# The low parts of the stick-breaking queries and keys: from VectorE to GpSimd

## The chip, the cores and the metric

The kernel runs on one core of a Trainium2 chip. A core has five engines that run side by side and meet only at semaphores: TensorE (PE in the profile, with its weight loads as PEld), VectorE (DVE), ScalarE (ACT), GpSimd (POOL) and SyncE (SP), which here only issues DMAs. The metric is the device time of one launch in microseconds (us); less is better.

## The reference

One decoder layer on 1024 tokens of width 1024. Attention has two groups of heads beside each other: 8 stick-breaking heads of 64 columns and 4 softmax heads (multi-head latent attention, MLA). The change touches the stick-breaking heads:

```python
z = einsum('bthd,bshd->bhts', q_block, k[:, :kend]) * 64 ** -0.5
strict = s_idx < t_idx
log_beta = log_sigmoid(z)
log_1m = where(strict, log_sigmoid(-z), 0.0)
after = cumsum(log_1m, reverse=True) - log_1m
w = where(strict, exp(log_beta + after), 0.0)
out_block = w @ v[:, :kend]
```

All is float32. The output projection and a SwiGLU feed-forward layer follow.

## The kernel before

Products with float32 accuracy are made of rounded parts. ScalarE copies an operand into a tile of type fp32r (the high part), and another engine subtracts that from the operand (the low part). Three products of parts, or for the 64-column stick heads two products with stacked parts, then stand for one.

The attention stage works in units. A unit is one head and one block of 128 queries; BLOCKS says how many blocks of 128 keys it meets (1, 7, 3, 5, 6, 4, 8, 2, in this order, for each head). 16 units make a pair of heads. First come the 32 MLA units (2 pairs), then the 64 stick units (4 pairs). For each stick unit:

- TensorE makes the scores into PSUM (stick_scores, L1681 and L1682) from headQ, headKH and headKL;
- ScalarE makes omb = sigmoid(-z) (L783) and beta = sigmoid(z) (L791);
- VectorE makes left, a running product of omb (the scan of L1243), then beta = beta * left (the multiply of L1248), both on SBUF tiles;
- TensorE transposes beta (L1722), ScalarE copies it out (L727), TensorE multiplies with the values (L1735), and VectorE copies the output out of PSUM every fourth unit (L1234).

TensorE runs in the order: scores of unit n + 2, transposes of n, values of n - 1.

Each pair of heads needs its queries and keys in parts before its first unit. ScalarE writes pairQH (L735) and pairKH (L739) into one set of tiles; VectorE writes pairQL (L1186) and pairKL (L1190). For pair 0 this happens at unit 12 of the last MLA pair (SPLIT0), queries and keys together. For pairs 1 to 3 it happens during the pair ahead, queries at its unit 4 (SB_Q), keys at its unit 6 (SB_K), behind that unit's own work. SP's stack_head (L369 to L376) waits for all four parts (s_h and s_l) and copies them with five DMAs per head into headQ, headKH and headKL. TensorE waits for the DMAs (head_in) at the first unit of a head. For pairs 1 to 3, SP issues only after the scores of unit 7 (head 0) or 15 (head 1) of the pair ahead.

GpSimd has little to do here: it zeroes the other half of headKL (L522) and the first column of left (L525), and comes back only when the attention is over (L530).

Of the kernel before, what the change touches and what calls it, by code (L numbers as in the profile page):

```python
# [19 lines left out]
ALU = mybir.AluOpType  # L20
# [8 lines left out]
SBH, SBD = 8, 64  # L29
# [74 lines left out]
SB_Q, SB_K, SB_OUT = 4, 6, 11  # L104
# [5 lines left out]
def build(nc, xT, cols_d, rows_d, grow_d, pos_d, ada1_d, ada2_d, win_d, qup_d, kvup_d, wout_d, gu_d, down_d, x2_d, t_d, out_d):  # L110
# [3 lines left out]
    def at(name, shape, dt, kb):  # L114
        return nc.alloc_sbuf_tensor_at(name, shape, dt, offset=base + int(kb * 1024))
# [39 lines left out]
    qkT = at("qkT", [P, 8, S], F32, 34)  # L155
# [45 lines left out]
    pairQH = at("pairQH", [P, S], F32R, 106)  # L201
    pairQL = at("pairQL", [P, S], F32R, 110)
    pairKH = at("pairKH", [P, S], F32R, 114)
    pairKL = at("pairKL", [P, S], F32R, 118)
# [68 lines left out]
    sem = {n: ctx.enter_context(nc.semaphore(n)) for n in names}  # L273
# [53 lines left out]
    def repeat(eng, n, body):  # L327

        if n == 1:
            body(0)  # L330
        else:
            with eng.Fori(0, n) as i:
                body(i)
# [123 lines left out]
    @block.gpsimd  # L457
    def _(pool):
        for n in ("q_r", "rk_done"):
            pool.sem_inc(sem[n], PRIME)  # L460
        k = 0

        def fill(ins):
            nonlocal k
            ins.then_inc(sem["pool_const"], 1)
            k += 1

        fill(pool.memset(ident[:], 0.0))
        fill(pool.memset(identb[:], 0.0))
        fill(pool.memset(mask_sb[:], 0.0))  # L470
        fill(pool.memset(mask_mla[:], 0.0))
        fill(pool.memset(ones[:], 1.0))
        fill(pool.memset(nhalf[:], -0.5))
        pool.wait_ge(sem["pool_const"], k)
        for m in (ident, identb):
            fill(pool.affine_select(out=m[:], in_=m[:], compare_op=ALU.not_equal, fill=1.0, base=0, pattern=[[-1, P]], channel_multiplier=1))

        fill(pool.affine_select(out=mask_sb[:], in_=mask_sb[:], compare_op=ALU.is_gt, fill=NEG, base=0, pattern=[[1, P]], channel_multiplier=-1))
        fill(pool.affine_select(out=mask_mla[:], in_=mask_mla[:], compare_op=ALU.is_ge, fill=NEG, base=0, pattern=[[1, P]], channel_multiplier=-1))

        def rsqrt(k, row, t0=0, t1=NT):

            pool.wait_ge(sem["stat_ms"], k + 1)
            nc.gpsimd.tensor_tensor(rms[:, row, t0:t1], ms[:, row, t0:t1], nhalf[:, t0:t1], ALU.pow).then_inc(sem["stat_r"], 1)

        pool.wait_ge(sem["pool_const"], k)
        rsqrt(0, 0)

        for j in range(KD):
            pool.wait_ge(sem["hH_done"], j + 1)  # L490
            nc.gpsimd.tensor_tensor(hL[:, j, :], x_in[:, j, :], hH[:, j, :], ALU.subtract).then_inc(sem["hL_done"], 1)

        pool.wait_ge(sem["hL_done"], KD)
        pool.memset(acc2[:], 0.0).then_inc(sem["ada_acc"], 1)

        for k, (a, b) in enumerate(((0, 1), (0, 2), (1, 2))):
            pool.wait_ge(sem["low_sq"], (2, 3, 5)[k])
            if k:
                pool.wait_ge(sem["low_add"], k)
            nc.gpsimd.tensor_tensor(sql[a][:], sql[a][:], sql[b][:], ALU.add).then_inc(sem["low_add"], 1)  # L500
        rsqrt(1, 1)
        rsqrt(2, 2)

        def head_rsqrt(i):
            for u in range(2):
                tt = 2 * i + u
                pool.wait_ge(sem["q_ms"], tt + 1)
                nc.gpsimd.tensor_tensor(rstd[:, u, 0:4], qms[:, u, 0:4], nhalf[:, 0:4], ALU.pow).then_inc(sem["q_r"], 1)  # L508
                pool.wait_ge(sem["k_ms"], tt + 1)
                nc.gpsimd.tensor_tensor(rstd[:, u, 4:9], qms[:, u, 4:9], nhalf[:, 0:5], ALU.pow).then_inc(sem["rk_done"], 1)  # L510
        repeat(pool, NT // 2, head_rsqrt)

        pool.wait_ge(sem["low_over"], 1)
        for e in range(2):
            o = 64 * (1 - e)
            pool.memset(KRH[e][o:o + 64, :].bitcast(F32), 0.0).then_inc(sem["kr_zero"], 1)
            pool.memset(KRL[e][o:o + 64, :].bitcast(F32), 0.0).then_inc(sem["kr_zero"], 1)

        for e, u in ((0, NU + 7), (1, 2 * NU - 1)):
            pool.wait_ge(sem["m_qk"], after(u))  # L520
            o = 64 * (1 - e)
            pool.memset(headKL[e][o:o + 64, :].bitcast(F32), 0.0).then_inc(sem["sk_zero"], 1)  # L522
            pool.wait_ge(sem["sk_zero"], e + 1)
        for s in range(2):
            pool.memset(left[s][:, 0:1], 1.0).then_inc(sem["left_one"], 1)  # L525
        pool.wait_ge(sem["left_one"], 2)

        for tt in range(NT):
            pool.wait_ge(sem["o_ms"], tt + 1)
            nc.gpsimd.tensor_tensor(ors[:, ORDER0[tt], :], oms[:, ORDER0[tt], :], nhalf[:, 0:2], ALU.pow).then_inc(sem["o_r"], 1)  # L530

        pool.wait_ge(sem["mix_l"], NT)
        pool.memset(sqa[:], 0.0).then_inc(sem["sqa_zero"], 1)
        for hf in range(2):
            rsqrt(3 + hf, 3, 4 * hf, 4 * hf + 4)

        for hf in range(2):
            if hf == 0:
                pool.wait_ge(sem["g_mm"], NQ * NSU)
                pool.wait_ge(sem["x2_spill"], 16)  # L540
            else:
                pool.wait_ge(sem["y_done"], KD)
            pool.dma_start(xres[:], x2_d[:, :, 512 * hf:512 * hf + 512].rearrange("j p n -> p j n")).then_inc(sem["xres_in"], 16)
            for o in range(KD):
                pool.wait_ge(sem["y_done"], hf * KD + o + 1)
                pool.dma_start(out_d[o, :, 512 * hf:512 * hf + 512], yst[:, o, :]).then_inc(sem["y_out"], 16)
            pool.wait_ge(sem["y_out"], 16 * KD * (hf + 1))
# [382 lines left out]
    def _(dve):  # L930
        for n in ("q_free", "kr_free", "work_done", "t_dve", "m_max", "m_nm", "m_tv", "m_o", "s_scan", "s_wd", "s_o", "t_done", "ll_done", "x2_done", "sqa_done"):
            dve.sem_inc(sem[n], PRIME)
        V = nc.vector
# [247 lines left out]
                n0, n = G0[v] * P, BLOCKS[v] * P  # L1181
                V.tensor_copy(pmT[v % 2][:, n0:n], ps[:, 5, 0:n - n0]).then_inc(sem["m_tv"], 1)

        def stick_q(p):
            dve.wait_ge(sem["s_h"], 2 * p + 1)
            V.tensor_tensor(pairQL[:], qkT[:, p, :], pairQH[:], ALU.subtract).then_inc(sem["s_l"], 1)  # L1186

        def stick_k(p):
            dve.wait_ge(sem["s_h"], 2 * p + 2)
            V.tensor_tensor(pairKL[:], qkT[:, 4 + p, :], pairKH[:], ALU.subtract).then_inc(sem["s_l"], 1)  # L1190

        def maxima(done, recips):

            return min(done, NM) + recips + PRIME
# [10 lines left out]
        def mla_step(u):  # L1205

            p, v = divmod(u, NU)
            n = BLOCKS[v] * P
            dve.wait_ge(sem["m_qk"], after(u))
            V.reduce_max(mx[:, v:v + 1], pair(2 * (v % 2), n), axis=AX.X).then_inc(sem["m_max"], 1)  # L1210
            dve.wait_ge(sem["m_max"], maxima(u + 1, max(0, u - 3)))
            V.tensor_scalar(nmx[:, v:v + 1], mx[:, v:v + 1], -(QK ** -0.5), None, ALU.mult).then_inc(sem["m_nm"], 1)
            if u >= 2:
                mla_copy((u - 2) // NU, (u - 2) % NU)
            if u >= 3:
                mla_finish(u - 3)
            if v == SPLIT1:
                mla_split(p, 1)
            if v == SPLIT0:
                if p == 0:  # L1220
                    mla_split(1, 0)
                else:
                    stick_q(0)
                    stick_k(0)

        def stick_output(u):

# [8 lines left out]
        def stick_step(u):  # L1236

            i, v = divmod(u, NU)
            last = i == SBH // 2 - 1
            n = BLOCKS[v] * P  # L1240
            dve.wait_ge(sem["s_nb"], after(u))
            dve.wait_ge(sem["s_wd"], after(u - 2))
            V.tensor_tensor_scan(left[v % 2][:, 1:n], omb[v % 2][:, 0:n - 1], omb[v % 2][:, 0:n - 1], 1.0, ALU.mult, ALU.bypass).then_inc(sem["s_scan"], 1)  # L1243
            if u < 2:
                mla_copy(MH // 2 - 1, NU - 2 + u)
            dve.wait_ge(sem["s_b"], after(u))
            dve.wait_ge(sem["s_scan"], after(u))
            V.tensor_tensor(beta[v % 2][:, 0:n], beta[v % 2][:, 0:n], left[v % 2][:, 0:n], ALU.mult).then_inc(sem["s_wd"], 1)  # L1248
            if u < 3:
                mla_finish(NM - 3 + u)  # L1250
            else:
                stick_output(u - 3)
            if v == SB_Q and not last:
                stick_q(i + 1)
            if v == SB_K and not last:
                stick_k(i + 1)
            if last and SB_OUT <= v < SB_OUT + 2:
                wsplit(H_OUT + v - SB_OUT, H_OUT + v - SB_OUT)

# [17 lines left out]
        for tt in range(NT + 1):  # L1277
# [6 lines left out]
            if tt >= 1:  # L1284
                k = tt - 1
# [719 lines left out]
```

## Time and profile before

| | |
|---|---|
| median of 3 runs | 1446.08 us (1443.46 to 1449.19) |
| the profiled execution | 1443.19 us |
| its span, first to last instruction | 1441.20 us |
| TensorE busy | 1326.0 us, 92% |
| VectorE busy | 833.1 us, 58% |
| ScalarE busy | 547.3 us, 38% |
| GpSimd busy | 84.5 us, 6% |
| mean granted TensorE clock | 0.971 |
| the stick-breaking stage | about 461 to 634 us of the span |

A timeline row reads: start, duration, engine, line of the kernel, operation, output <- inputs, how many, and in brackets the idle time before it with what ended it. An instruction may be issued before the one ahead has drained, so neighbours can overlap by 0.1 us. "issue" means that the wait isn't explained by what the profile records of engines; a wait for a DMA can hide there.

### The profile page before, as it was taken

Reading aid. Unit: us, or ns where it says so; the run is one execution under the profiler, and the core shown is the slowest. Engines: PE = TensorE matmul, PEld = TensorE weight load, DVE = VectorE, ACT = ScalarE, POOL = GpSimd, SP = SyncE. Lnnn points to the kernel's source line nnn. Section 1 sums busy time; section 2 is a strip of 40 time slices with the busy share of each in tenths; the row PEclk is TensorE's granted clock in tenths of the full one; section 3 lists DMA queues with packets and bytes.
Section 4 is the critical chain, followed back from the end, with each engine's and each line's share of the span. In section 5 each row is a group of like instructions: output and inputs, shape, how many; then the busy total and the mean of one; then the engine's idle time right before and its main releaser. Section 6 shows DMA issues by size and latency. Waiting matters only on the chain.

```text
span 1441.2 us, 17190 instructions
## 1 busy us (share of the span) xinstructions
PE 1326.0 (92%) x6624; PEld 1107.3 (77%) x6624; DVE 833.1 (58%) x1225; ACT 547.3 (38%) x883; POOL 84.5 (6%) x82
## 2 busy tenths in 40 slices
PE   2899999887989898969989999999999999999998
PEld 1688878776877777768867788888888877887886
DVE  8633354477565998865368755666566633334333
ACT  3522312356444776852136333333333322323231
POOL 1600200132000000010000000000000000001001
PEclk9799999899999999979999999999999999999999
DMA  9053423000003323500122122222222225446443
GB/s 383 31 212 124 161 102 121 15 0 1 1 1 74 76 50 74 183 30 17 57 99 106 74 88 88 88 88 88 88 74 74 72 77 201 154 137 242 161 146 124
DMA packets 37404, 143.47 MB, mean 100 GB/s; under 512 B 4176, under 2 KB 4304, under 8 KB 35792
## 3 DMA queue, kind: packets, MB, share of 16 engines
q1 hardware_dynamic: 34992, 134.03, 27.5%
q0 software_dynamic: 2336, 8.39, 1.6%
q8 instruction: 52, 0.85, 0.3%
q14 instruction: 24, 0.20, 0.0%
HBM read 112.00 MB, written 19.92 MB: 92 GB/s over the span
## 4 chain that ended last, share of the span: by engine, by line
PE 71%; DVE 16%; issue 6%; ACT 3%; POOL 2%; DMA 1%; DVEq 0%; SPq 0%; ACTq 0%; POOLq 0%
PE ps L1905 26%; PE ps L1517 15%; PE ps L1506 8%; PE ps L1508 8%; PE ps L1507 8%; DVE left L1243 5%; PE ps L1713 2%; DVE acc L995 1%; DVE beta L1248 1%; PE ps L1702 1%; POOL rstd L508 1%; PE ps L1735 1%; PE ps L1722 1%; DMA t_spill_d<-tst 1%; PE ps L1822 1%
## 5 line engine op out<-in xcount | busy, mean ns | idle before, releaser
L1506 PE MATMUL ps<-TH,dWH 128*128 128x512 f32 x352 | 137.8, 391 | 7.2 <-DVE dWL L1474 6.3
L1507 PE MATMUL ps<-TL,dWH 128*128 128x512 f32 x352 | 137.7, 391 | 0.0
L1508 PE MATMUL ps<-TH,dWL 128*128 128x512 f32 x352 | 137.6, 391 | 0.0
L1905 PE MATMUL ps<-h2H,slH 128*128 128x512 f32 x320 | 124.6, 389 | 2.4 <-ACT s L900 2.4
L1905 PE MATMUL ps<-h2L,slH 128*128 128x512 f32 x320 | 124.5, 389 | 0.0
L1905 PE MATMUL ps<-h2H,slL 128*128 128x512 f32 x320 | 124.5, 389 | 0.0
L1472 DVE TENSOR_TENSOR TL<-traw,TH 128x512 fp32r<-128x512 f32 x44 | 30.5, 693 | 138.6 <-ACT TH L921 138.6
L883 ACT ACTIVATE slH<-ssum 128x512 fp32r<-128x512 f32 x80 | 50.4, 632 | 146.3 <-PE ps L1905 96.2
L1243 DVE TENSOR_TENSOR_SCAN left<-omb 128x127 f32<-128x127 f32 (+3 forms) x64 | 86.3, 1348 | 13.7 <-ACT omb L783 13.7
L921 ACT ACTIVATE TH<-traw 128x512 fp32r<-128x512 f32 x44 | 27.8, 631 | 168.9 <-PE ps L1508 156.8
L974 DVE TENSOR_TENSOR WL<-raw,WH 128x1024 fp32r<-128x1024 f32 x30 | 38.3, 1280 | 85.9 <-ACT WH L561 85.9
L1506 PEld LDWEIGHTS ps<-TH,dWH 128*128 128x128 f32 x352 | 66.5, 189 | 22.3 <-issue 7.1
L1517 PE MATMUL ps<-hH,WH 128*128 128x512 f32 x256 | 79.6, 392 | 0.0
L1517 PE MATMUL ps<-hL,WH 128*128 128x512 f32 x256 | 78.9, 389 | 0.0
L1517 PE MATMUL ps<-hH,WL 128*128 128x512 f32 x256 | 78.8, 389 | 0.0
L1508 PEld LDWEIGHTS ps<-TH,dWL 128*128 128x128 f32 x352 | 66.5, 189 | 13.8
L1507 PEld LDWEIGHTS ps<-TL,dWH 128*128 128x128 f32 x352 | 66.4, 189 | 13.8
L1735 PE MATMUL ps<-VS,wT 128*128 128x64 f32 x576 | 75.1, 278 | 0.0
L1735 PEld LDWEIGHTS ps<-VS,wT 128*128 128x128 f32 x576 | 73.4, 201 | 0.0
L1905 PEld LDWEIGHTS ps<-h2H,slH 128*128 128x128 f32 x320 | 60.1, 188 | 15.3 <-DVE slL L1419 2.8
L1905 PEld LDWEIGHTS ps<-h2L,slH 128*128 128x128 f32 x320 | 60.1, 188 | 12.4
L1905 PEld LDWEIGHTS ps<-h2H,slL 128*128 128x128 f32 x320 | 60.1, 188 | 12.4
(296 smaller groups left out, 3021.3 us busy)
## 6 DMA issues: line engine op xcount, KB each, us to landing
ada<-ada SPq DMA_DIRECT2D x12, 2048.0 KB, 8.1
draw<-down SPq DMA_DIRECT2D x44, 512.0 KB, 3.6
sraw<-gu SPq DMA_DIRECT2D x20, 1024.0 KB, 5.9
traw<-t_spill_d SPq DMA_DIRECT2D x44, 256.0 KB, 3.8
t_spill_d<-tst SPq DMA_DIRECT2D x20, 512.0 KB, 3.0
raw<-win SPq DMA_DIRECT2D x18, 512.0 KB, 3.7
x_in<-xT SPq DMA_DIRECT2D x4, 1024.0 KB, 8.5
headKH<-pairKH SPq DMA_DIRECT2D x16, 256.0 KB, 4.9
```

Source lines behind the costliest of these rows:

```text
L883: A(slH[q][:], operand(u, q), ACT.Copy).then_inc(sem["g_h"], 1)
L921: A(TH[d % 2][:], traw[d % 2][:], ACT.Copy).then_inc(sem["th_done"], 1)
L974: V.tensor_tensor(WL[par % 2][:], raw[r % 2][:], WH[par % 2][:], ALU.subtract).then_inc(sem["split_l"], 1)
L1243: V.tensor_tensor_scan(left[v % 2][:, 1:n], omb[v % 2][:, 0:n - 1], omb[v % 2][:, 0:n - 1], 1.0, ALU.mult, ALU.bypass).then_inc(sem["s_sca ...
L1472: V.tensor_tensor(TL[d % 2][:], traw[d % 2][:], TH[d % 2][:], ALU.subtract).then_inc(sem["tl_done"], 1)
L1506: mm(out, lh, rh, start=first, stop=False)
L1507: mm(out, lh, rl, start=False, stop=False)
L1508: return mm(out, ll, rh, start=False, stop=last)
L1517: last = mm(ps[:, b + hf, :], l[s][:, j * P:(j + 1) * P], r[:, j, 512 * hf:512 * hf + 512], start=(j == 0 and k == 0), stop=(j == KD - 1 a ...
L1713: last = mm(ps[:, 6 + v % 2, 0:VD], pmT[v % 2][:, k * P:(k + 1) * P], VM[:, qt + k, (2 * i + e) * VD:(2 * i + e + 1) * VD], start=(k == 0) ...
L1735: last = mm(ps[:, bank, c:c + SBD], wT[v % 2][:, k * P:(k + 1) * P], VS[:, qt + k, (2 * i + e) * SBD:(2 * i + e + 1) * SBD], start=(k == 0 ...
L1905: last = mm(ps[:, Q_BANK[q], :], l[q][:, w], r[:, c, :], start=(c == 0 and k == 0 and q not in (Q_G2, Q_S4)), stop=(c == 3 and k == 2), sk ...
```

## The change

The two helper functions of VectorE, stick_q and stick_k, and their calls are gone. GpSimd gets stick_lows(p): for the queries and then the keys of pair p it waits for ScalarE's high part and subtracts. Pair 0's are made right after the first headKL memset, pairs 1 to 3's after the left memsets, each as soon as its high part is there. ScalarE, SP and TensorE are untouched; SP still waits for the same counts of s_l.

```diff
+        def stick_lows(p):
+
+            for k, (lo, hi, x) in enumerate(((pairQL, pairQH, qkT[:, p, :]), (pairKL, pairKH, qkT[:, 4 + p, :]))):
+                pool.wait_ge(sem["s_h"], 2 * p + k + 1)
+                nc.gpsimd.tensor_tensor(lo[:], x, hi[:], ALU.subtract).then_inc(sem["s_l"], 1)
+
         for e, u in ((0, NU + 7), (1, 2 * NU - 1)):
             pool.wait_ge(sem["m_qk"], after(u))
             o = 64 * (1 - e)
             pool.memset(headKL[e][o:o + 64, :].bitcast(F32), 0.0).then_inc(sem["sk_zero"], 1)
             pool.wait_ge(sem["sk_zero"], e + 1)
+            if e == 0:
+                stick_lows(0)
         for s in range(2):
             pool.memset(left[s][:, 0:1], 1.0).then_inc(sem["left_one"], 1)
         pool.wait_ge(sem["left_one"], 2)
+        for p in range(1, SBH // 2):
+            stick_lows(p)
...
-        def stick_q(p):
-            dve.wait_ge(sem["s_h"], 2 * p + 1)
-            V.tensor_tensor(pairQL[:], qkT[:, p, :], pairQH[:], ALU.subtract).then_inc(sem["s_l"], 1)
-
-        def stick_k(p):
-            dve.wait_ge(sem["s_h"], 2 * p + 2)
-            V.tensor_tensor(pairKL[:], qkT[:, 4 + p, :], pairKH[:], ALU.subtract).then_inc(sem["s_l"], 1)
-
...
             if v == SPLIT0:
                 if p == 0:
                     mla_split(1, 0)
-                else:
-                    stick_q(0)
-                    stick_k(0)
...
-            if v == SB_Q and not last:
-                stick_q(i + 1)
-            if v == SB_K and not last:
-                stick_k(i + 1)
```

## Rows read from the trace of the kernel before

**Rows 1.** The page's first part: busy time of each engine.
```profile
PE 1326.0 (92%) x6624; PEld 1107.3 (77%) x6624; DVE 833.1 (58%) x1225; ACT 547.3 (38%) x883; POOL 84.5 (6%) x82
```
**Rows 2.** VectorE's timeline in the stick-breaking stage.
```profile
473.35 1.75 DVE L1243 TENSOR_TENSOR_SCAN left<-omb 128x767 f32<-128x767 f32 x1
475.20 0.96 DVE L1248 TENSOR_TENSOR beta<-beta,left 128x768 f32<-128x768 f32 x1
476.08 1.22 DVE L1186 TENSOR_TENSOR pairQL<-qkT,pairQH 128x1024 fp32r<-128x1024 f32 x1
...
479.14 2.28 DVE L1243 TENSOR_TENSOR_SCAN left<-omb 128x1023 f32<-128x1023 f32 x1
481.53 1.23 DVE L1248 TENSOR_TENSOR beta<-beta,left 128x1024 f32<-128x1024 f32 x1
...
483.01 1.21 DVE L1190 TENSOR_TENSOR pairKL<-qkT,pairKH 128x1024 fp32r<-128x1024 f32 x1
...
486.73 2.02 DVE L1243 TENSOR_TENSOR_SCAN left<-omb 128x895 f32<-128x895 f32 x1 [0.65 <-ACT omb L783]
...
506.30 2.02 DVE L1243 TENSOR_TENSOR_SCAN left<-omb 128x895 f32<-128x895 f32 x1 [1.27 <-ACT omb L783]
...
527.00 2.02 DVE L1243 TENSOR_TENSOR_SCAN left<-omb 128x895 f32<-128x895 f32 x1 [0.65 <-ACT omb L783]
...
569.74 2.02 DVE L1243 TENSOR_TENSOR_SCAN left<-omb 128x895 f32<-128x895 f32 x1 [2.87 <-ACT omb L783]
```
**Rows 3.** The chain that ended last: start, us, what ran on it.
```profile
476.08 1.22 DVE pairQL L1186
...
481.53 1.24 DVE beta L1248
482.81 1.09 PE ps L1722 x8
```
**Rows 4.** VectorE's timeline at places where GpSimd also worked.
```profile
39.44 2.34 DVE L1021 TENSOR_TENSOR x_in<-x_in,ps 128x1024 f32<-128x1024 f32 x2
...
42.47 2.73 DVE L995 SCALAR_TENSOR_TENSOR acc<-ada,silu_c,acc 128x512 f32<-128x512 f32 x1
...
147.16 1.65 DVE L974 TENSOR_TENSOR WL<-raw,WH 128x1024 fp32r<-128x1024 f32 x1 [8.10 <-ACT WH L561]
...
167.98 2.58 DVE L974 TENSOR_TENSOR WL<-raw,WH 128x1024 fp32r<-128x1024 f32 x1 [6.01 <-ACT WH L561]
```
**Rows 5.** GpSimd's timeline at the same places.
```profile
39.78 2.37 POOL L491 TENSOR_TENSOR hL<-x_in,hH 128x1024 fp32r<-128x1024 f32 x1 [14.60 <-ACT hH L579]
42.11 2.54 POOL L491 TENSOR_TENSOR hL<-x_in,hH 128x1024 fp32r<-128x1024 f32 x1
...
145.32 2.41 POOL L500 TENSOR_TENSOR sql<-sql,sql 128x1024 f32<-128x1024 f32 x1 [72.77 <-ACT sql L602]
147.87 3.19 POOL L500 TENSOR_TENSOR sql<-sql,sql 128x1024 f32<-128x1024 f32 x1
...
167.08 2.40 POOL L500 TENSOR_TENSOR sql<-sql,sql 128x1024 f32<-128x1024 f32 x1 [16.02 <-ACT sql L602]
```
**Rows 6.** SP's timeline: the last copy issued for head 0.
```profile
455.21 1.23 SPq L376 DMA_DIRECT2D headKL<-pairKL  x1
```
**Rows 7.** headKL's view between 455 and 456 us: that copy alone.
```profile
DMA to landing us min/median/max: 6.0/6.0/6.0
```
**Rows 8.** TensorE's timeline: the first matmul of the stick-breaking stage.
```profile
461.26 0.30 PE L1681 MATMUL ps<-headKH,headQ 128*128 128x128 f32 x1 [2.50 <-issue]
```
**Rows 9.** ScalarE's timeline: the high parts for pair 1.
```profile
473.31 1.09 ACT L735 ACTIVATE pairQH<-qkT 128x1024 fp32r<-128x1024 f32 x1
...
478.74 1.06 ACT L739 ACTIVATE pairKH<-qkT 128x1024 fp32r<-128x1024 f32 x1
```
**Rows 10.** VectorE's timeline: the low part of pair 0's queries.
```profile
449.60 1.22 DVE L1186 TENSOR_TENSOR pairQL<-qkT,pairQH 128x1024 fp32r<-128x1024 f32 x1 [0.98 <-ACT pairQH L735]
```
**Rows 11.** Windows: busy time and count of each engine, PEclk, DMA share, GB/s.
```profile
562.00:564.00 2.00, 0.71 (x4) 0.66 (x4) 1.94 (x3) 0.28 (x1) 0.00 (x0) 0.62 0.03 8
```

## The prediction

> **What bounds the kernel now.** I read the page's first part first: TensorE (PE) is busy 92% of the span, VectorE (DVE) 58%, GpSimd (POOL) 6% [rows 1]. That is a mean over stages, so the stage that the change touches has to be read by itself. In VectorE's timeline of the stick-breaking stage [rows 2] the reader sees that one scan starts when the multiply before it ends and the multiply when its scan ends: 473.35 + 1.75 = 475.10, multiply at 475.20, and so on. VectorE has hardly a gap in eight units, and the chain of waits goes through its scans and multiplies, and through pairQL at 476.08 [rows 3]. So this stage is VectorE's. The one place where it is not is the end of each run of eight units: the multiply of 1024 columns at 481.53 is followed on the chain by PE's transposes (482.81), values and scores, ScalarE's (ACT) sigmoid omb, and only then VectorE's scan at 486.73, which has waited 0.65 us for omb [rows 2, 3]. Between 482.76 and 486.73 VectorE has slack.
>
> At the entrance of the stage something else rules. PE's first stick matmul is at 461.26, after 2.50 us for which no engine is named [rows 8]. The last copy of head 0's operands was issued at 455.21 and took 6.0 us to land [rows 6, 7]: 455.21 + 6.0 = 461.2. PE waits for that DMA, which waits for both low parts.
>
> **The change part by part.**
>
> *Two subtractions leave VectorE in each of three pairs.* I take the start of the 895-column scan as the mark of a run of eight units [rows 2]. 486.73 to 506.30, without low parts: 19.57 us. 506.30 to 527.00, with both: 20.70 us. The difference is 1.13 us, about one subtraction and not two. pairQL (1.22 us, 1.14 start to start) is on the chain. pairKL at 483.01 lies in the slack behind the 1024 multiply: it costs nothing now. So the removal gives 3 x 1.13 = 3.4 us, and only for the query parts.
>
> *The same subtractions on GpSimd.* Its subtractions and additions of 128x1024 f32 take 2.40 us alone (167.08) [rows 5], twice VectorE's 1.22. That alone would be hidden: the low parts of pair 1 are wanted by a DMA issued about 20 us before PE needs them. What is not hidden is what happens to VectorE beside them. VectorE's WL subtraction at 167.98 has pairQL's shape and took 2.58 us, not 1.22; it began inside the GpSimd operation 167.08 to 169.48. The one at 147.16 took 1.65 us, with GpSimd's operation ending at 147.73 [rows 4, 5]. Both fit one formula: VectorE loses (end of GpSimd's operation - own start - 0.14): 169.48 - 167.98 - 0.14 = 1.36 = 2.58 - 1.22; 147.73 - 147.16 - 0.14 = 0.43 = 1.65 - 1.22. It does nothing until GpSimd is through. The reverse holds too: GpSimd's second addition at 147.87 took 3.19 us, ending 2.25 us after VectorE's end at 148.81. VectorE's stream of close instructions is no shelter: its acc operation at 42.47, half the size, took 2.73 us, ending 0.55 after GpSimd's subtraction of 42.11 to 44.65. Between a scan and its multiply there is a gap of 0.10 us (475.10 to 475.20) in which a waiting GpSimd can start. An operation with an input in PSUM is not held: the two x_in sums at 39.44 took 2.34 us together beside GpSimd's at 39.78 [rows 4, 5].
>
> The beta multiply (beta times left) has two SBUF inputs like WL's subtraction, so it will be held. Whether the scan holds GpSimd off, and is held, no row shows. Two bounds. ACT's pairQH ends at 473.31 + 1.09 = 474.40 [rows 9], in the middle of a scan.
> - If the scan excludes GpSimd, GpSimd starts when the scan ends (475.10), ends 2.23 later at 477.33, and the multiply due at 475.20 loses 477.33 - 475.20 - 0.14 = 1.99. For the key part, ACT's pairKH ends at 479.80, that is 3.64 us after the end of the multiply at 475.20 + 0.96; ACT follows that multiply by a transpose, a copy and a sigmoid, so the distance stays. Without pairQL's 1.14 the 1023-column scan runs from 479.14 - 476.16 - 1.14 = 1.84 to 4.12 us after that multiply, and the 1024 multiply is due at 481.53 - 476.16 - 1.14 = 4.23 [rows 2]. So GpSimd again asks inside a scan and enters in the gap before the 1024 multiply: 1.99 again. That multiply is on the chain [rows 3].
> - If the scan leaves GpSimd alone, it starts at once (474.45, to 476.83): the first multiply loses 476.83 - 475.20 - 0.14 = 1.49; the second, due 4.23 after the mark with GpSimd ending at 3.69 + 2.38 = 6.07, loses 1.70.
>
> Per pair that is 1.99 + 1.99 - 1.13 = 2.85 by the first, 1.49 + 1.70 - 1.13 = 2.06 by the second; three pairs, 8.6 or 6.2. I take the first: the scan's operands lie in SBUF as two inputs (omb given twice), which is what the held rows have in common against the PSUM ones. Below these bounds would be GpSimd yielding always; that is a rival.
>
> The Trainium skill, SBUF — State Buffer, section "Who interferes with whom", says it as a rule: a VectorE instruction with two SBUF inputs contends with a GpSimd instruction that reads SBUF, and the later one blocks fully. It speaks against this change. The rows on tensor_tensor agree (1.36 and 0.43 us lost). Applied to the scan it would give the 8.6 and not the 6.2; a reader who ignores the page has both ends above.
>
> *The first pair.* Its low parts ran on VectorE from 449.60, and SP could issue when the second ended at about 451.97 [rows 6, 10]. On GpSimd two operations take 4.8 us (2 x 2.40) from 449.6, so 454.4: 2.4 us later. All of it goes to the landing that PE waits for (461.26 becomes 463.7). VectorE's 2.4 us that become free lie in the softmax stage, ahead of a PE that then waits for the DMA anyway: worth nothing. VectorE's operations there read PSUM or one column; if one were held, then until 454.4 at most, and PE, which was through by 458.76, has 4.9 us of idle time to take it. Cost +2.4; bounds 0 (if PE's stall has another cause) and 2.8.
>
> *Queues.* GpSimd's memset of headKL's second half stands behind the new operations till 454.4, but its own condition, the scores of the last MLA unit, comes in PE's order just ahead of the stall that began at 461.26 - 2.50 = 458.76 [rows 8]. SP's head copies: for pairs 1 to 3 the key part is ready about where it was, since the VectorE version ran after the 1024 multiply and the new one before it; PE wants the copies nearly 20 us later. Nothing is added there.
>
> *TensorE's clock.* The stalls leave PE without work for 2.0 us more before each of the 1024 unit's transposes and for 4.9 instead of 2.50 us at the entrance. In this trace the granted clock between 562 and 564 was 0.62, a mean of 2.4 and 1.2 GHz, and PE had been busy for only 0.71 of those 2 us, waiting before such transposes [rows 11]. VectorE's next 895-column scan then waited 2.87 us for omb, not 0.65, and the two runs of eight from 527.00 to 569.74 took 42.74 against 20.70 + 19.57 = 40.27: a low stretch on the chain costs 2.5 us [rows 2]. The runs ending at 486.73, 506.30 and 527.00 show none. With longer stalls I expect more low stretches: one more than before as the likeliest, 2.5 us; bounds -2.5 (none at all) and +7.5 (the entrance and all three pairs).
>
> **Sum.** -3.39 (query parts) + 11.94 (six held multiplies of 1.99) + 2.4 (entrance) + 2.5 (clock) = +13.5 us. The profiled execution took 1443.19 us (span 1441.20 and 1.99 around it), so it would give 1456.7. It lies 2.9 us under the median of the three runs, 1446.08, to which I add the same: 1459.6.
>
> **Rivals.**
> 1. The scan does not take part: 6.2 + 2.4 + 2.5 = +11.1, and without the extra low stretch +8.6: 1454.7 to 1457.2. For it: no row has a scan beside GpSimd. Against it: two SBUF inputs.
> 2. GpSimd yields: it runs only where VectorE is idle or reads PSUM, so that no multiply waits. Then -3.4 + 2.4 = -1.0: 1445.1, no difference. VectorE's idle time behind the 1024 multiply is 0.65 us with pairKL and about 1.1 more without, less than the 2.4 needed, and the rows at 42.47 and 167.98 show VectorE waiting. This is the case on the other side (not slower). It decides from the point where the six multiplies lose under 1.3 us each instead of 1.99.
> 3. The clock falls at every stall: +11.0 + 7.5 = +18.5, 1464.6.
> 4. The entrance is not bound by the DMA: 2.4 less, 1457.2. It changes the size, not the sign.
> 5. Faster: GpSimd yields and the entrance costs nothing, -3.4: 1442.7, which is still within 0.5%. Only with the clock's low stretch gone too (-5.9) is it near 0.4%.
>
> **How the numbers follow.** A difference under 0.5% (7.2 us) can hardly be told from none here. My forecast, both multiplies held and one low stretch more, give or take, has 0.58, with its own range 1455 to 1464. Rival 1 has 0.17, rival 3 0.08, rival 4 is in the forecast's range, rival 2 0.13, anything faster 0.04. Slower by over 0.5% begins at 1453.3: 0.58 + 0.08 + most of 0.17 = 0.82. Within 0.5%: 0.14. The range leaves out rival 2 and the faster cases (0.17) and little above: from 1451, rival 1 less half the spread of the runs shown (1443.46 to 1449.19), to 1466, rival 3 and a bit.
>
> **What would show it.** In the new trace: six multiplies (768 and 1024 columns, in pairs 0 to 2) about 2 us longer than their 0.96 and 1.23 us, each beside a GpSimd subtraction that begins at a scan's end; the run of eight with low parts at 19.6 + 4.0 us; SP's first head copy at 454.4; PE's first stick matmul at 463.7; unchanged time elsewhere. If the multiplies keep their length, the lock is wrong and so is the forecast. If GpSimd's subtractions start inside scans at once and take 2.4 us, rival 1 is right.

## The result, and the profile after

The change makes the kernel slower. The median of four runs is 1466.41 us (1465.00 to 1466.97), that of the kernel before is now, with a fourth run, 1447.63 us (1446.08 when the forecast was made); the ratio is 1.0128 with a 95% interval of 1.0107 to 1.0150. That is +18.8 us, where +13.5 was forecast and the range ended 0.4 us under the measured median. The profiled execution took 1466.97 us with a span of 1465.1.

First VectorE's timeline of pair 0, the stretch that answers to [rows 2].

```profile
477.48 1.75 DVE L1242 TENSOR_TENSOR_SCAN left<-omb 128x767 f32<-128x767 f32 x1
479.33 2.88 DVE L1247 TENSOR_TENSOR beta<-beta,left 128x768 f32<-128x768 f32 x1
482.13 1.21 DVE L1242 TENSOR_TENSOR_SCAN left<-omb 128x511 f32<-128x511 f32 x1
483.45 0.69 DVE L1247 TENSOR_TENSOR beta<-beta,left 128x512 f32<-128x512 f32 x1
484.06 2.28 DVE L1242 TENSOR_TENSOR_SCAN left<-omb 128x1023 f32<-128x1023 f32 x1
486.44 3.12 DVE L1247 TENSOR_TENSOR beta<-beta,left 128x1024 f32<-128x1024 f32 x1
...
496.01 2.02 DVE L1242 TENSOR_TENSOR_SCAN left<-omb 128x895 f32<-128x895 f32 x1 [2.87 <-ACT omb L793]
```

GpSimd's timeline beside it.

```profile
449.44 2.40 POOL L523 TENSOR_TENSOR pairQL<-qkT,pairQH 128x1024 fp32r<-128x1024 f32 x1 [19.23 <-ACT pairQH L745]
451.78 2.40 POOL L523 TENSOR_TENSOR pairKL<-qkT,pairKH 128x1024 fp32r<-128x1024 f32 x1
...
478.66 2.73 POOL L523 TENSOR_TENSOR pairQL<-qkT,pairQH 128x1024 fp32r<-128x1024 f32 x1 [21.57 <-ACT pairQH L745]
485.92 2.55 POOL L523 TENSOR_TENSOR pairKL<-qkT,pairKH 128x1024 fp32r<-128x1024 f32 x1 [4.53 <-ACT pairKH L749]
```

The two subtractions are off VectorE, and two multiplies have become longer: 2.88 us for 768 columns and 3.12 for 1024, against 0.96 and 1.23 [rows 2]. GpSimd's operation of 478.66 ends at 481.39, 2.16 us after the end of the scan (479.23); that of 485.92 ends at 488.47, 2.13 after its scan (486.34). Both are recorded from inside a scan, but by their ends they ran after it: alone one takes 2.40. So the scan keeps GpSimd out, and GpSimd then keeps the multiply out.

Rows of TensorE's timeline: the entrance, which answers to [rows 8], then the transposes of the 768 and the 1024 unit in pair 0, of the 1024 unit in pair 1 and of both in pair 2.

```profile
463.39 0.44 PE L1676 MATMUL ps<-headKH,headQ 128*128 128x128 f32 x1 [4.91 <-issue]
...
482.27 0.87 PE L1717 MATMUL ps<-ident,beta 128*128 128x128 f32 x6 [2.02 <-DVE beta L1247]
...
489.61 1.97 PE L1717 MATMUL ps<-ident,beta 128*128 128x128 f32 x8 [3.02 <-DVE beta L1247]
...
536.93 1.97 PE L1717 MATMUL ps<-ident,beta 128*128 128x128 f32 x8 [3.02 <-DVE beta L1247]
...
575.00 0.88 PE L1717 MATMUL ps<-ident,beta 128*128 128x128 f32 x6 [1.84 <-DVE beta L1247]
...
582.36 1.97 PE L1717 MATMUL ps<-ident,beta 128*128 128x128 f32 x8 [0.90 <-DVE beta L1247]
```

The stall at the entrance is 4.91 us (4.9 forecast, 2.50 before), and the one ahead of the 1024 unit's transposes 3.02 in pair 0 (1.29 before). Ahead of the 768 unit's six transposes there are now 2.02 us, where PE did not wait at all before. The eight transposes of the 1024 unit take 1.97 us, where the chain of the kernel before had 1.09 [rows 3]. The windows say why (PE, PEld, DVE, ACT and POOL busy, then PEclk, DMA share, GB/s).

```profile
482.00:486.00 4.00, 3.73 (x34) 3.69 (x35) 3.90 (x4) 2.82 (x5) 0.08 (x1) 1.00 0.00 0
486.00:490.00 4.00, 0.98 (x8) 0.85 (x8) 3.90 (x4) 1.05 (x4) 2.48 (x1) 0.76 0.08 18
490.00:494.00 4.00, 4.00 (x19) 3.48 (x18) 1.54 (x4) 1.19 (x2) 0.00 (x0) 0.50 1.02 211
494.00:498.00 4.00, 4.00 (x20) 3.90 (x19) 1.99 (x1) 2.00 (x3) 0.00 (x0) 0.50 0.48 98
```

PE was busy 0.98 of 4 us, and from there the clock is at 0.50, 1.2 GHz, for more than 8 us. The stall ahead of the 768 unit, 2.02 us, did not lower it: from 482 to 486 us it is 1.00, and those six transposes take 0.87 us, the old length. The 895-column scan at 496.01 waited 2.87 us for omb.

**Where the time went**, between the two profiled spans (1441.20 and 1465.1, 23.9 apart; the one before, 1443.19 us, is 4.4 us under the median of its kernel). The marks are the starts of the 895-column scans, as in the prediction. Seven runs of eight units lie between the first and the last mark:

| from mark to mark, us | before | after | difference |
|---|---|---|---|
| 1: low parts of pair 1 inside | 21.28 | 26.43 | +5.15 |
| 2 | 19.57 | 21.46 | +1.89 |
| 3: low parts of pair 2 | 20.70 | 25.86 | +5.16 |
| 4 | 19.56 | 19.56 | 0.00 |
| 5: low parts of pair 3 | 23.18 | 25.87 | +2.69 |
| 6 | 19.56 | 22.56 | +3.00 |
| 7 | 19.56 | 19.57 | +0.01 |

The sum is +17.9. The six held multiplies are 11.4 us of it, the absent query subtractions -3.4, and 9.9 us are left. They are the clock: run 3 after should be 19.57 + 1.92 + 1.89 = 23.38 and is 25.86; runs 2 and 6, with no low part in them, are longer because the low stretch goes on into them (the last one to about 598 us, 9 us behind its mark of 588.76). The entrance adds 4.1 more up to the first mark: the stall is 2.4 of it, and from the first stick matmul to the mark there are 6.19 us and not 4.19, 2.0 more, at the low clock. The last 1.9 us lie behind the last mark and are not explained here.

### The profile page after: what moved, and what is told of

The parts are those of the page before. It is cut to its first block, busy times and chain, and to the rows that moved or that the text cites. A ratio compares the mean times of both kernels' runs of the same rounds, so it can differ in the third digit from the quotient of the medians.

```text
span 1465.1 us, 17190 instructions
## 1 busy us (share of the span) xinstructions
PE 1343.6 (92%) x6624; PEld 1122.8 (77%) x6624; DVE 836.2 (57%) x1217; ACT 547.3 (37%) x883; POOL 104.8 (7%) x90
## 4 chain that ended last, share of the span: by engine, by line
PE 72%; DVE 15%; issue 6%; ACT 3%; POOL 2%; DMA 1%; DVEq 0%; SPq 0%; ACTq 0%; POOLq 0%
PE ps L1900 25%; PE ps L1512 15%; PE ps L1501 8%; PE ps L1503 8%; PE ps L1502 8%; DVE left L1242 4%; PE ps L1708 2%; PE ps L1730 2%; DVE beta L1247 1%; DVE acc L1005 1%; PE ps L1717 1%; PE ps L1697 1%; POOL rstd L508 1%; PE ps L1676 1%; DVE sqs L990 1%
## 5 line engine op out<-in xcount | busy, mean ns | idle before, releaser
L1730 PE MATMUL ps<-VS,wT 128*128 128x64 f32 x576 | 82.0, 295 | 0.0
L1730 PEld LDWEIGHTS ps<-VS,wT 128*128 128x128 f32 x576 | 80.7, 218 | 0.0
L1717 PE MATMUL ps<-ident,beta 128*128 128x128 f32 x288 | 49.5, 305 | 22.7 <-DVE beta L1247 21.3
L1900 PEld LDWEIGHTS ps<-h2H,slL 128*128 128x128 f32 x320 | 60.3, 189 | 12.7
```

The costliest lines, as they stand in the source:

```text
L1717: last = nc.tensor.transpose(ps[:, 4 + k // 4, k % 4 * P:(k % 4 + 1) * P], beta[v % 2][:, k * P:(k + 1) * P], ident[:])
L1730: last = mm(ps[:, bank, c:c + SBD], wT[v % 2][:, k * P:(k + 1) * P], VS[:, qt + k, (2 * i + e) * SBD:(2 * i + e + 1) * SBD], start=(k == 0 ...
L1900: last = mm(ps[:, Q_BANK[q], :], l[q][:, w], r[:, c, :], start=(c == 0 and k == 0 and q not in (Q_G2, Q_S4)), stop=(c == 3 and k == 2), sk ...
```

## The experiments

The theory: GpSimd's read of SBUF holds the multiply, for as long as GpSimd's instruction lasts, and PE's longer stalls lower its clock. The rivals: only the entrance costs, results are late, any work on GpSimd disturbs, or the clock doesn't matter.

### Each half of the change alone

Pair 0 alone on GpSimd (p0_gp): VectorE gets its two helpers and their calls for pairs 1 to 3 back.

```diff
-        for p in range(1, SBH // 2):
-            stick_lows(p)
...
+            if v == SB_Q and not last:
+                stick_q(i + 1)
+            if v == SB_K and not last:
+                stick_k(i + 1)
```

> Pair 0's low parts alone on GpSimd; pairs 1 to 3 stay on VectorE. Entrance theory: PE waits for head 0's copies and these for the low parts, so the stall before the first stick matmul is 4.9 us and not 2.5, and the clock falls in it: +2.4 for the stall and about +1.7 for the matmuls behind it at the low clock, +4 us in all, no multiply longer than before. Rival (the entrance is not bound by the low parts): 0 us. Rival (the whole loss comes from the entrance): +18.

Measured: 1454.25 us against 1447.89, ratio 1.0040 (1.0025 to 1.0055). No multiply is longer. So this half costs some 6 us by the medians, more than the 2.4 us of the stall.

```profile
465.38 0.45 PE L1686 MATMUL ps<-headKH,headQ 128*128 128x128 f32 x1 [4.96 <-issue]
```

The trace shows 4.5 of them at the entrance: 2.46 us in the stall (4.96 against 2.50) and 2.0 at the low clock behind it (the first mark comes 6.20 us after this matmul, against 4.19). In this profile one more low stretch than in the kernel before lies between the marks, behind the 1024 multiply of 590.60 in pair 2; it makes runs 6 and 7 2.3 and 3.3 us longer, although no multiply there is. Whether it has to do with the entrance is not shown.

Pairs 1 to 3 alone (p13_gp): stick_lows(0) taken out and VectorE's calls for pair 0 put back.

> Pairs 1 to 3 alone on GpSimd; pair 0 stays on VectorE. Port theory: six multiplies longer by 1.9 us (+11.4), three query subtractions gone from the chain (-3.4), and a low stretch of the clock behind each 1024 multiply where the kernel before had one in its profile (+5 to +7.5): +13 to +16 us. Rival (only the lateness of the low parts matters): 0 to -3. With the run of pair 0 alone the two should add up to the whole change, about +19.

Measured: 1461.76 us, ratio 1.0091 (1.0063 to 1.0120), +13.9. The two halves give 0.0040 + 0.0091 = 0.0131, the whole 0.0128.

### Work on GpSimd that nobody waits for

The kernel before, with six GpSimd operations at the moments at which the change has its own. In dummy_read they read SBUF, in dummy_write they only write.

```diff
+        for p in range(1, SBH // 2):
+            for k in range(2):
+                if 2 * (p - 1) + k:
+                    pool.wait_ge(sem["dummy"], 2 * (p - 1) + k)
+                pool.wait_ge(sem["s_h"], 2 * p + k + 1)
+                nc.gpsimd.tensor_tensor(scratch[:, 0:S], qkT[:, p, :], qkT[:, 4 + p, :], ALU.subtract).then_inc(sem["dummy"], 1)
```

> The kernel before, and beside it six GpSimd subtractions of two SBUF tiles of 128x1024 into a scratch tile that nobody reads, begun at the moments at which the change begins its own for pairs 1 to 3. All low parts stay on VectorE. Port theory: the same multiplies take 2.9 and 3.1 us, +11.5 from them and up to +7.5 from the clock, so +13 to +19 us although no result is late. Rival (the loss comes from results that are late, or from the changed order on VectorE): 0 us.

> As the run with dummy subtractions, but the GpSimd work is a memset of 128x2560 (about 2.3 us, by the 3.5 us for 128x4096 in the trace): as long, but it reads nothing in SBUF. If GpSimd holds VectorE through what it reads, the multiplies keep 0.96 and 1.23 us and the time stays within 2 us of before. Rival (any GpSimd work on SBUF holds VectorE): +13 to +19 as with the subtractions.

Measured: reading, 1462.87 us, ratio 1.0109 (1.0077 to 1.0141). Writing, 1447.39 us, ratio 0.9997 (0.9978 to 1.0016). VectorE's multiplies of pair 0 with the reading dummy:

```profile
476.59 2.87 DVE L1256 TENSOR_TENSOR beta<-beta,left 128x768 f32<-128x768 f32 x1
479.39 1.21 DVE L1194 TENSOR_TENSOR pairQL<-qkT,pairQH 128x1024 fp32r<-128x1024 f32 x1
...
484.83 3.11 DVE L1256 TENSOR_TENSOR beta<-beta,left 128x1024 f32<-128x1024 f32 x1
```

and with the writing one, GpSimd's row and VectorE's:

```profile
478.79 2.24 POOL L533 MEMSET scratch<- 128x2560 f32 x1 [18.03 <-ACT pairQH L742]
```
```profile
479.48 0.96 DVE L1255 TENSOR_TENSOR beta<-beta,left 128x768 f32<-128x768 f32 x1
```

The same 2.87 and 3.11 us without any result being late or any order changed, and 0.96 beside a memset that runs from 478.79 to 481.03. So lateness, order and the mere presence of GpSimd work are out: work that reads SBUF holds the multiply, and work that only writes doesn't. (The two dummies differ in the operation too, a subtraction and a memset, so the reading isn't separated from the rest of the subtraction.) In the profile of the writing dummy the clock fell behind two of the three 1024 multiplies with low parts, although they were not longer; the kernel before has that behind one of three.

### Queries alone, keys alone

Of pairs 1 to 3 one kind goes to GpSimd (with a count of its own, for which SP waits), the other stays on VectorE.

> Of pairs 1 to 3 the queries' low parts alone on GpSimd, keys and pair 0 on VectorE. Port theory: three multiplies of 768 columns longer by 1.9 us, three subtractions gone: 3 x (1.9 - 1.1) = +2.3 us, and up to +5 more if the clock falls behind these multiplies too. Rival (moving the queries' part gains, and the loss is all from the keys): -3.

> Of pairs 1 to 3 the keys' low parts alone on GpSimd. They lay in VectorE's slack, so nothing is gained: 3 x 1.9 = +5.7 us from the 1024 multiplies, and +5 to +7.5 from the clock in the longer stall before the transposes: +8 to +13. With the queries' run it should add up to the +14 of pairs 1 to 3. Rival (key parts are as free on GpSimd as they were on VectorE): 0.

Measured, with 1444.13 us for the kernel before: queries 1454.64 us, ratio 1.0080 (1.0053 to 1.0107), keys 1456.65 us, ratio 1.0077 (1.0053 to 1.0100). By the medians that is +10.5 and +12.5 us, by the ratios +11.6 and +11.1. The keys are as expected. The queries cost +10.5, far over the +2.3 and over the +7 with the clock, and the two add up to 0.0157, where both together cost 0.0091: some 9.5 us too much, within wide intervals. The trace of the queries' run shows what I had left out (VectorE, then PE):

```profile
519.60 2.87 DVE L1260 TENSOR_TENSOR beta<-beta,left 128x768 f32<-128x768 f32 x1
...
533.18 0.29 DVE L1260 TENSOR_TENSOR beta<-beta,left 128x128 f32<-128x128 f32 x1 [2.20 <-ACT beta L803]
535.43 2.02 DVE L1255 TENSOR_TENSOR_SCAN left<-omb 128x895 f32<-128x895 f32 x1 [1.96 <-ACT omb L795]
```
```profile
522.52 1.13 PE L1732 MATMUL ps<-ident,beta 128*128 128x128 f32 x6 [1.84 <-DVE beta L1260]
...
530.01 1.92 PE L1732 MATMUL ps<-ident,beta 128*128 128x128 f32 x8
```

PE's stall of 1.84 us before the six transposes is followed by the low clock, which lasts over the whole chain behind the 1024 multiply: those transposes start at 530.01, when the multiply had ended at 527.93, and take 1.92 us. This run of eight takes 535.43 - 510.42 = 25.01 us where 19.57 + 1.91 = 21.5 is due. With both kinds on GpSimd the same run takes 25.86 us (run 3 of the table), only 0.85 more. One held multiply can be enough to bring the low clock over the chain of its run of eight, and a second shares it. (It isn't always: of the three pairs of q_gp two have these 25 us, and in the changed kernel the clock stayed up behind the 768 unit's stalls of pairs 0 and 1, 2.02 and 1.84 us.) The sharing is part of why the halves don't add up. In the profiles the low clock adds 8.7 us to the seven runs in q_gp, 9.4 in k_gp, 12.7 in p13_gp and 2.5 in the kernel before; over the kernel before that is 6.2 + 6.9 against 10.2, about 3 of the 9.5 us. The rest isn't located.

### GpSimd's work in pieces

SP waits for four times the count.

```diff
-                nc.gpsimd.tensor_tensor(lo[:], x, hi[:], ALU.subtract).then_inc(sem["s_l"], 1)
+                for c in range(4):
+                    w = slice(256 * c, 256 * c + 256)
+                    nc.gpsimd.tensor_tensor(lo[:, w], x[:, w], hi[:, w], ALU.subtract).then_inc(sem["s_l"], 1)
```

> The changed kernel with each GpSimd subtraction cut into four of 256 columns. Theory (held for one whole GpSimd instruction, handed over between instructions): no VectorE instruction loses more than about 0.5 us at a time, the queries still cost about 2 us in sum, spread over four instructions, the keys only their first piece or two before the 1024 multiply, the rest falls into the slack, and the stall that lowers the clock is shorter: 4 to 10 us under the changed kernel, 1456 to 1462. Rival (a queue of GpSimd work goes first as a whole): 1466 and multiplies of about 3 us.

Measured: 1457.79 us, ratio 1.0094 (1.0073 to 1.0116), 8.6 us under the changed kernel by the medians. The kernel before stood at 1444.13 us beside this run and at 1447.63 beside the changed kernel; by the ratios (1.0094 and 1.0128) the gain is only 4.9 us, still inside what was expected. VectorE's rows:

```profile
478.33 1.24 DVE L1249 TENSOR_TENSOR beta<-beta,left 128x768 f32<-128x768 f32 x1
479.50 1.75 DVE L1244 TENSOR_TENSOR_SCAN left<-omb 128x511 f32<-128x511 f32 x1
481.35 0.97 DVE L1249 TENSOR_TENSOR beta<-beta,left 128x512 f32<-128x512 f32 x1
482.24 2.81 DVE L1244 TENSOR_TENSOR_SCAN left<-omb 128x1023 f32<-128x1023 f32 x1
485.15 1.50 DVE L1249 TENSOR_TENSOR beta<-beta,left 128x1024 f32<-128x1024 f32 x1
```

Four pieces on GpSimd, in the softmax stage and then beside these instructions:

```profile
450.72 2.82 POOL L525 TENSOR_TENSOR pairKL<-qkT,pairKH 128x256 fp32r<-128x256 f32 x4
...
477.66 5.24 POOL L525 TENSOR_TENSOR pairQL<-qkT,pairQH 128x256 fp32r<-128x256 f32 x4 [22.05 <-ACT pairQH L747]
```

Each instruction loses 0.27 to 0.54 us, scans too: 1.75 against 1.21 for 511 columns, 2.81 against 2.28 for 1023. Four pieces take 5.24 us there and not 2.82. The two engines take turns by instruction. The queries' pieces cost 0.28 + 0.54 + 0.28 + 0.53 = 1.63 us on a chain from which 1.13 went. The stalls before the 1024 unit's transposes are 2.1 us, and the clock still falls in all three pairs; at the entrance the pieces make the stall longer, 5.73 us.

### The clock by itself

Matmuls whose result is overwritten, put into PE's stalls: as shown before the transposes, and by the same helper before the first stick scores.

```diff
+        def keep_busy(bank, n):
+            for _ in range(n):
+                mm(ps[:, bank, :], VS[:, 0, 0:P], VS[:, 0, :], start=True, stop=True)
...
-            pe.wait_ge(sem["s_wd"], after(u))
             pe.wait_ge(sem["s_ta"], after(u - 1))
+            keep_busy(4, FILL.get((i, v), 0))
+            pe.wait_ge(sem["s_wd"], after(u))
```

> The changed kernel with matmuls whose result is overwritten put into TensorE's stalls: 16 before the first stick matmul, 6 before the transposes of unit 4 and 10 before those of unit 6, in pairs 0 to 2. If the low clock behind the stalls costs time, the low stretches there vanish and the time falls by 2 us for each of the four, 8 us or so, to 1457 to 1460, with the multiplies still 2.9 and 3.1 us. Rival (the low clock is no cause, or costs nothing on the chain): 1466 or more.

Measured: 1486.60 us, ratio 1.0292 (1.0271 to 1.0313). The expectation was wrong by my sizes: each float32 product runs as two matmuls of 0.43 us, so the 16 at the entrance took 13.90 us in a stall of 4.9. It says nothing on the question.

> The first filler run put 13.9 us of matmuls (0.43 us for each half of a float32 product) into a stall of 4.9, so it could not tell. Here the fillers fit: 5 products (4.3 us) at the entrance, 2 (1.7) before the transposes of unit 4, 3 (2.6) before those of unit 6. If the low clock behind the stalls costs 1.7 us at the entrance and 2.5 in each of the three pairs, about 8 us come back: 1457 to 1460. Rival (low clock off the chain): 1465 or more.

Measured: 1454.71 us, ratio 1.0050 (1.0033 to 1.0068): 11.7 us under the changed kernel by the medians, more than expected. VectorE and the windows there:

```profile
479.18 2.88 DVE L1248 TENSOR_TENSOR beta<-beta,left 128x768 f32<-128x768 f32 x1
...
486.29 3.12 DVE L1248 TENSOR_TENSOR beta<-beta,left 128x1024 f32<-128x1024 f32 x1
...
493.39 2.02 DVE L1243 TENSOR_TENSOR_SCAN left<-omb 128x895 f32<-128x895 f32 x1 [1.27 <-ACT omb L794]
```
```profile
486.00:490.00 4.00, 3.82 (x16) 1.90 (x16) 3.90 (x4) 0.90 (x3) 2.33 (x1) 1.00 0.14 31
490.00:494.00 4.00, 4.00 (x36) 3.69 (x33) 2.01 (x5) 2.76 (x5) 0.00 (x0) 1.00 0.97 202
```

The multiplies are as long as in the changed kernel (2.88 and 3.12), the clock stays at 1.00, and the scan waits 1.27 us and not 2.87. The runs with low parts of pairs 2 and 3 now take 23.38 and 23.39 us: what the held multiplies alone make of 19.57. The profiled execution is the slowest of the nine, and one low stretch was left in it, from 594 to 610 us, where no filler stood: runs 6 and 7 took 21.56 and 22.95 us. So the low clock is on the chain, and it comes from the stalls.

### The entrance, and a version that beats both

The changed kernel with pair 0's high parts at unit 10 of the last MLA pair (ScalarE's calls moved; GpSimd follows).

> The changed kernel with the high parts of pair 0 (and so GpSimd's low parts) made at unit 10 of the last softmax pair and not at unit 12, some 7 us earlier. If the entrance costs because PE waits for the copies behind GpSimd, the stall of 4.9 us nearly goes, and the low clock behind it: -6 us against the changed kernel, 1460. Rival (another cause for the stall): no change.

Measured: 1459.60 us, ratio 1.0081 (1.0052 to 1.0110), 6.8 under the changed kernel by the medians. PE's first stick matmul starts at 458.82, right behind the last of the ones ahead, and the first mark follows 4.19 us later, at the full clock.

The other way round: the kernel before, everything on VectorE, with pair 0's parts at unit 10 too and the query subtraction where VectorE has slack.

```diff
             if v == SB_K and not last:
+                stick_q(i + 1)
                 stick_k(i + 1)
-            if v == SB_Q and not last:
-                stick_q(i + 1)
```

> The kernel before, all low parts on VectorE, with two moves: pair 0's parts at unit 10 and not 12 (takes away the 2.5 us stall at the entrance), and the queries' subtraction of pairs 1 to 3 put behind unit 6, next to the keys', where VectorE has about 1.8 us of slack for 2.3 us of work (0.6 us gained each instead of 1.1 lost). -2.5 - 1.9 = -4.4 us, and up to -3 more if shorter stalls keep the clock up: 0.3 to 0.5% faster than before. Rival (the slack is needed by something else): -2.5 or 0.

Measured: 1440.42 us against 1446.75, ratio 0.9954 (0.9935 to 0.9972). VectorE behind the 1024 multiply:

```profile
480.96 1.23 DVE L1247 TENSOR_TENSOR beta<-beta,left 128x1024 f32<-128x1024 f32 x1
482.10 0.42 DVE L1233 COPY o_sb<-ps 128x256 f32<-128x256 f32 x1
482.43 1.22 DVE L1186 TENSOR_TENSOR pairQL<-qkT,pairQH 128x1024 fp32r<-128x1024 f32 x1
483.56 1.22 DVE L1190 TENSOR_TENSOR pairKL<-qkT,pairKH 128x1024 fp32r<-128x1024 f32 x1
...
486.56 2.02 DVE L1242 TENSOR_TENSOR_SCAN left<-omb 128x895 f32<-128x895 f32 x1
```

Both subtractions lie in the slack, and the scan follows without idle time. The run of eight from 506.12 takes 19.98 us: 0.4 more than one without low parts, where the kernel before has 1.13 more.

With one filler product before the transposes of units 6 and 14 as well (best):

> As the run with both moves, plus one float32 product whose result is overwritten (0.87 us) before the transposes of units 6 and 14 of every pair, where PE waits 1.1 to 1.3 us for VectorE's 1024 multiply. If PE's stall there is what lets the clock fall now and then, this gives 2 us or so more for each stretch avoided. Rival (0.87 us of filler changes nothing, or delays the transposes): equal or slower than without.

Measured: 1434.15 us, ratio 0.9910 (0.9889 to 0.9931), with 6.3 us between the two. 0.87 us of otherwise useless matmuls pays. In the profile of slack_early the clock fell twice in the stage, from 560 to 566 and from 622 us on; with the filler it is 1.00 up to 630 us, where the last stick unit's matmuls are over:

```profile
460.00:631.00 171.00, 158.78 (x1198) 132.62 (x1196) 149.78 (x177) 131.74 (x238) 3.69 (x7) 1.00 0.37 95
```

## Why the prediction was right or wrong

**What bounds the stage: right.** The chain goes through scans and multiplies; the keys' part in the slack was free on VectorE [rows 2, 3], and slack_early shows that the queries' can be nearly free there too.

**The removal, -3.4: right** in place and size; the sum of run 3 in after_fill2 (23.38) uses it.

**The held multiplies, +11.9: right.** 11.4 measured, six times 1.89 to 1.92 for a forecast 1.99. The formula from [rows 4, 5] holds to the hundredth (481.39 - 479.33 - 0.14 = 1.92; 488.47 - 486.44 - 0.14 = 1.89); only its input was 0.1 us too long, as a GpSimd operation that has waited ended 2.16 and 2.13 us after VectorE's and not 2.23 (the prediction's own row has 2.25). Of the two bounds, the one in which the scan takes part is shown, in both directions: it keeps GpSimd out (after) and is held by it (pieces). With that rival 1 falls. The Trainium skill's rule (SBUF — State Buffer, "Who interferes with whom": a VectorE instruction with two SBUF inputs contends with a GpSimd instruction that reads SBUF, not with one that only writes) is borne out for multiply and scan, and its last clause by dummy_read (1.0109) against dummy_write (0.9997). Rival 2, GpSimd yielding, falls by every multiply.

**The entrance, +2.4: right** as a stall (4.91 against 2.50 us; first copy issued at 454.25, 454.4 forecast), and rival 4 falls by after_early. The 2.0 us at the low clock behind it belong to the next term.

**The clock, +2.5: this is the step that failed.** I had the mechanism and its price behind a single stall, and took one more low stretch than before as the likeliest, where rival 3, with its +7.5 and 1464.6 us, got 0.08. Three things were wrong.

- How many stretches. Between the marks the kernel before has one low stretch in its profile; the changed kernel has one in each of the pairs 0 to 2, and a fourth at the entrance. [rows 11] showed the clock falling already after a stall of about 1.3 us, in one of the pairs; stalls of 3.0 and 4.9 us should have moved the weight to all of them.
- Which stalls. The term has only the stalls at the entrance and before the 1024 unit's transposes. Those before the 768 unit's transposes, 1.84 to 2.02 us where there was none, got no clock at all. In pair 2 the low stretch began behind that one (575.00, at 577 us the clock is 0.50), and q_gp, where no other stall is longer, cost +10.5 for the +2.3 without the clock.
- The price of a stretch. I took the 2.5 us of one that ended within its run of eight; here two of them lasted on into the next runs, which became 1.9 and 3.0 us longer.

In place of the +2.5 the profiles show 9.9 us between the marks and 2.0 at the entrance. By the medians the clock is what is left: 18.8 - (11.4 - 3.4 + 2.4) = 8.4 us. The profile of the kernel before lies 4.4 us under its median and that of the changed kernel 0.6 over its own, so the medians leave less. after_fill2 gives back 11.7 (11.3 by the ratios), the low stretches that the kernel before has too among them.

**The range** ended at 1466 because rival 3 was cut short ("and a bit"). With the 1.9 and 3.0 us of the longer stretches on top of its 1464.6 it would have reached 1469.5; that is hindsight. The miss by 0.4 us is narrow: on the later median of the kernel before, 1447.63, the same range would have ended at 1467.5 and held. That would have been luck, as the clock's term was too small by a factor of three or more. **The sign** and its chance of 0.82 were right.

Open: what decides behind which of two equal stalls the clock falls, where the last 1.9 us of the two profiles lie, and how much more than the 8.4 after_fill2 would gain over a kernel before without low stretches.

## What to carry to other kernels

Before moving an elementwise operation to an idle GpSimd, look at what VectorE does in that stretch: if its instructions read two SBUF tiles, they and a GpSimd operation that reads SBUF take turns by whole instructions, and GpSimd's turn was twice as long here (2.40 us against 1.22). Look first for slack on VectorE itself, here behind the one unit whose result the other engines must bring back. And price a stall of TensorE with the low clock that follows: a few us of throw-away matmuls that surely fit into the stall can show what the clock costs, and can pay.

## What the runs showed of the hardware that I had not expected

- One stall of 1.84 us was followed by some 10 us at the low clock (q_gp, two pairs of three), and either kind alone cost nearly as much as the two together (q_gp 1.0080, k_gp 1.0077, both 1.0091).
- Equal stalls do not have equal effects. In the kernel before PE waits 1.29 us at 482.81, 523.08 and 563.34, and the clock falls only at the third. At the entrance, with 2.4 to 2.6 us of stall, the first mark comes 4.19 us after the first stick matmul in two profiles (before, p13_gp) and 5.7 to 5.8 in four (dummy_read, dummy_write, q_gp, k_gp). So a single profile is a poor measure of what the low clock costs a kernel.
- 0.87 us of matmuls inside stalls of 1.1 to 1.6 us kept the clock at 2.4 GHz through the stage in the profile: 6.3 us of 1440 by the medians.
- A GpSimd memset of 128x2560 (2.24 us) left VectorE's multiplies at 0.96 and 1.23 us.
